# A two-layer transformer block on one core: the first layer's GpSimd work moved to VectorE and TensorE, and its bias table built from bfloat16 parts

## The chip, the cores and the metric

One core of a Trainium2 chip. The metric is the device time of one execution in microseconds (us); the kernel before has a median of 1634.03 us over 3 runs (1628.46 to 1635.84). A measurement of this kernel can tell about 0.5% (8 us) from no change.

## The reference

512 tokens of width 1024, two layers. What matters here, per layer:

```python
h = rmsnorm(x, norm_mix[l]);  proj = h @ w_in[l]
ua, cq, ckv, kr, qc, kc, vc, ud = jnp.split(proj, IN_SPLITS, axis=-1)
ya = conformer_conv(ua, ...)        # 31 taps over 512 tokens, 256 channels
yb = mla(cq, ckv, kr, ...)          # rope, causal attention, 4 heads
yc = diff_attention(qc, kc, vc, ..., rel_bias, ...)  # + rel_bias[t5_bucket(rel)]
yd = multiscale_pool(ud, ...)       # mean over windows of 2, 4, 8, 16 tokens, less u
x = x + concat([ya, yb, yc, yd]) @ w_out[l]
x = x + memory_cross_attention(rmsnorm(x), mem, ...)
x = x + conv_glu_ffn(rmsnorm(x), ...)
```

The bias `rel_bias[t5_bucket(rel)]` is the same in both layers. It is a sum of steps: for each of 31 distances at which the bucket changes, the difference of two rows of `rel_bias` times an indicator of 0 or 1.

## The kernel before

Everything is written by hand, engine by engine; each engine runs its own list in order and waits on counters (semaphores). x is kept transposed (channels on partitions) in eight tiles of 128 x 512.

**Matmuls.** A weight chunk `raw` (128 x 1024, two buffers) comes by DMA; ScalarE copies it to `wh` in the rounded type (`hi`, L534), VectorE makes the rest `wl` = raw - wh (`lo`, L888), and `gemm(n, ...)` does three products per 128 rows (L1344, L1346, L1347), 24 matmuls for a chunk n. `x` is split the same way into `a_hi` (ScalarE, L554) and `a_lo` (VectorE, L953). `gemm(n)` needs `lo(n)`, which VectorE does two chunks ahead, right after it has evicted chunk n-2 (`scaled`, L914). Chunks 0 to 14 are the projection, 15 to 30 the keys and values of the memory.

**Start of the first layer.** ScalarE squares the eight tiles of x into two buffers `sqx` (L557), GpSimd adds them up in `ssum` (L508), and TensorE makes the norm of it (`sums_of`, then `row_of` with the inverse root). VectorE makes the angles of rope between its `a_lo` (`reduce_angles`, L1007 to L1017).

**Bias table.** 16 tiles (`bias_tile(s)`, L1412), one after each projection chunk of the first layer. For each, ScalarE (5) and VectorE (3) make eight tiles of indicators 128 x 512 (`indicators`, L567 and L963) in one set of buffers, and TensorE does 8 float32 matmuls, 32 output columns each; four of them stand side by side in the array. One float32 matmul shows as two in the trace. ScalarE evicts the tile (`evict_bias`) and SyncE stores it to DRAM, from where the attention loads it in both layers.

**Projection loop.** For n = 0 to 11, VectorE does `scaled(n)`, `indicators(n + 2)` (first layer), `lo(n + 2)` and a number of the 62 convolution taps (`convolve`, L930, one 128 x 512 operation each). After n = 11 come four `qm` (L1074), which read the products `uq0` to `uq3` (L1377) out of two PSUM banks in turn; `uq1` waits until ScalarE has copied `kr` out (`km`, L642). GpSimd makes the window means of the pool branch (L459 to L480).

**Attention.** Steps t = 0 to 19; step t has scores of tile t (L1502 and L1510), softmax, and `gemm(15 + t)`. VectorE does in step 0 `negatives` (L1100), the remaining taps, then `lo(16)`; in step 1 `negatives`, the normalising, a further `negatives`, then `lo(17)`; and so on. TensorE asks for `lo(16)` at the beginning of step 1, between its scores.

Of the kernel before, what the change touches and what calls it, by code (L numbers as in the profile page):

```python
# [172 lines left out]
def block_program(nc, xT, memT, pos, const, vecs, small, w_first, w_main, w_up, w_down, w_last, out):  # L173
    with ExitStack() as ctx:
# [59 lines left out]
        ptr, _ = sb("ptr", [P, 4, 4, P], F32)  # L234
# [40 lines left out]
        assert at + 32 <= vc_at + 4096  # L275
# [3 lines left out]
        inds = [ering[:, i, :] for i in range(RING)] + [ptr[:, i].rearrange("p k q -> p (k q)") for i in range(2)]  # L279
# [11 lines left out]
        def v(name, j=0, w=1):  # L291
# [7 lines left out]
        bias0_in, mem_out, rope_in, masks = sem("bias0_in"), sem("mem_out"), sem("rope_in"), sem("masks_in")  # L299
        mem_sq, mem_root, mem_scaled = sem("mem_squared"), sem("mem_root"), sem("mem_scaled")  # L300
# [11 lines left out]
            "g_freed_by_act", "v_full", "v_freed_by_dve", "v_freed_by_act", "dve_steps", "pool_steps",  # L312
            "memf_in", "cross_maxima", "root_of_stat", "root_inverted", "gate_out", "pads_zeroed", "glu_done",
# [13 lines left out]
        DVE_INDS = ((0,), (1, 3))  # L327
        ACT_INDS = ((2, 4, 6), (5, 7))
        BIG = 2.0 ** 20

        def layer_program(layer):
# [3 lines left out]
             dve_steps, pool_steps, memf_in, xmax, root, root_inv, gate_out, pads, glu_done, cq_sq, m_hi, m_lo,  # L335
# [32 lines left out]
            def sync(sp):  # L368
# [56 lines left out]
                for n in range(4, 35):  # L425
# [3 lines left out]
                    if first and n == 12:  # L429
                        sp.wait_ge(mem_scaled, KT)  # L430
                        sp.dma_start(mem_norm, memf[:]).then_inc(mem_out, 16)
# [11 lines left out]
            def gpsimd(pool):  # L443
                step = Steps(pool, pool_steps)

# [6 lines left out]
                pool.wait_ge(pads, 2)  # L452

                def window_sums(i):

                    pool.wait_ge(g_dve, 8 + i)
                    u = ud[:, i, :]

                    step(pool.tensor_tensor(psa[:, 0:526], u[:, 1:527], u[:, 0:526], ALU.add))  # L459
                    if i == 0:  # L460
                        step(pool.tensor_tensor(psb[64:P, 0:524], psa[64:P, 2:526], psa[64:P, 0:524], ALU.add))
                    else:
                        step(pool.tensor_tensor(psb[:, 0:524], psa[:, 2:526], psa[:, 0:524], ALU.add))
                        step(pool.tensor_tensor(psa[:, 0:520], psb[:, 4:524], psb[:, 0:520], ALU.add))
                        step(pool.tensor_tensor(psb[64:P, 0:512], psa[64:P, 8:520], psa[64:P, 0:512], ALU.add))

                def window_differences(i):

                    u = ud[:, i, :]
                    if i == 0:  # L470
                        wins = ((slice(0, 64), psa, 14), (slice(64, P), psb, 12))
                    else:
                        wins = ((slice(0, 64), psa, 8), (slice(64, P), psb, 0))
                    for rows, win, o in wins:
                        inv16 = cst[rows, CCOLS["inv16"] + 16 * i:CCOLS["inv16"] + 16 * i + 16]
                        invw = cst[rows, CCOLS["invw"] + i:CCOLS["invw"] + i + 1]
                        pool.tensor_tensor(win[rows, o:o + 16], win[rows, o:o + 16], inv16, ALU.mult)
                        step(pool.tensor_scalar(win[rows, o + 16:o + S], win[rows, o + 16:o + S], invw, None,
                                                ALU.mult))
                        pool.tensor_tensor(u[rows, PPAD:PPAD + S], win[rows, o:o + S], u[rows, PPAD:PPAD + S],  # L480
                                           ALU.subtract).then_inc(ud_done, 1)
                    pool.wait_ge(ud_done, 2 * i + 2)
# [1398 lines left out]
```

## Time and profile before

| | |
|---|---|
| median of 3 runs | 1634.03 us |
| profiled execution | 1633.34 us, span 1631.6 us |
| TensorE busy | 1581.8 us (97%) |
| VectorE, ScalarE, GpSimd busy | 1024.8, 734.8, 196.9 us |
| mean granted TensorE clock | 0.982 of full |
| first layer, from the start to its attention | about 180 us |
| second layer, projection and attention begin | about 848 us, 954 us |

In the timelines a row merges neighbouring instructions of one line (xcount); "idle before" tells how long the engine had nothing and what released it. An instruction's duration contains its fill and drain, so the pace of a series is the distance of starts. The chain's rows count from the release on, without that overlap. PEclk 1.00 is 2.4 GHz, 0.50 is 1.2 GHz.

### The profile page before, as it was taken

To read this page: it belongs to the slowest core of one execution; us is meant where nothing else is said; L and a number is where in the kernel's file an instruction comes from. 1 tells how busy PE (TensorE), PEld (TensorE's weight loads), DVE (VectorE), ACT (ScalarE), POOL (GpSimd) and SP (SyncE) were. 2 spreads that over 40 slices of the span, in tenths; PEclk is the share of its full clock that TensorE was granted. 3 is DMA by queue.
4 is the path that set the end of the run, shared out by engine and by line. 5 is a ranking of instruction groups with operands and counts; after the bars stand their busy time and mean duration, and the time that the engine had idled before them with its cause. 6 is when DMAs were issued, how large, how long until landed. Compare 5 with 4: busy or idle time off the path is not lost.

```text
span 1631.6 us, 21648 instructions
## 1 busy us (share of the span) xinstructions
PE 1581.8 (97%) x7790; PEld 1229.9 (75%) x7790; DVE 1024.8 (63%) x1539; ACT 734.8 (45%) x1142; POOL 196.9 (12%) x140
## 2 busy tenths in 40 slices
PE   5999999999999999999999999999999999999997
PEld 3673677787688888888878677768768888888886
DVE  6698876543447746745767997654344773674574
ACT  6774767432444423423453266743244441442342
POOL 2050014220030000000021402422002000000002
PEclk7997999999999999999999999999999999999998
DMA  5232332132022323232243133212202323232322
GB/s 185 98 117 65 110 117 89 49 103 91 13 91 93 101 91 103 90 104 90 90 139 115 65 102 112 98 52 91 90 14 90 104 90 103 91 103 90 98 83 90
DMA packets 45437, 151.29 MB, mean 93 GB/s; under 512 B 5040, under 2 KB 5296, under 8 KB 44720
## 3 DMA queue, kind: packets, MB, share of 16 engines
q1 hardware_dynamic: 45360, 150.24, 27.8%
q8 instruction: 52, 0.85, 0.2%
q14 instruction: 25, 0.20, 0.0%
HBM read 142.88 MB, written 7.34 MB: 92 GB/s over the span
## 4 chain that ended last, share of the span: by engine, by line
PE 91%; DVE 4%; ACT 3%; issue 1%; DMA 1%; SPq 0%; DVEq 0%; ACTq 0%
PE psum L1344 25%; PE psum L1346 25%; PE psum L1347 25%; PE psum L1377 4%; PE psum L1524 2%; PE psum L1535 2%; PE psum L1502 2%; PE psum L1510 2%; PE psum L1412 2%; PE psum L1386 1%; PE psum L1398 1%; ACT wh L534 1%; DVE wl L888 1%; PE psum L1657 1%; ACT ering L806 0%
## 5 line engine op out<-in xcount | busy, mean ns | idle before, releaser
L534 ACT ACTIVATE wh<-raw 128x1024 fp32r<-128x1024 f32 x226 | 239.4, 1059 | 584.1 <-PE psum L1347 571.7
L1344 PE MATMUL psum<-a_hi,wh 128*128 128x512 f32 x1072 | 425.2, 397 | 10.2 <-DVE a_lo L953 10.1
L1346 PE MATMUL psum<-a_lo,wh 128*128 128x512 f32 x1072 | 420.6, 392 | 0.0
L1347 PE MATMUL psum<-a_hi,wl 128*128 128x512 f32 x1072 | 420.4, 392 | 0.0
L888 DVE TENSOR_TENSOR wl<-raw,wh 128x1024 fp32r<-128x1024 f32 x222 | 273.5, 1232 | 130.4 <-ACT wh L534 130.1
L1344 PEld LDWEIGHTS psum<-a_hi,wh 128*128 128x128 f32 x1072 | 203.4, 190 | 64.5 <-DVE a_lo L953 11.8
L1344 PE MATMUL psum<-b_hi,wh 128*128 128x512 f32 x608 | 240.4, 395 | 8.2 <-DVE x_sb L1222 4.4
L1347 PE MATMUL psum<-b_hi,wl 128*128 128x512 f32 x608 | 236.8, 389 | 0.0
L1346 PE MATMUL psum<-b_lo,wh 128*128 128x512 f32 x608 | 236.8, 389 | 0.0
L1347 PEld LDWEIGHTS psum<-a_hi,wl 128*128 128x128 f32 x1072 | 203.2, 190 | 43.3
L1346 PEld LDWEIGHTS psum<-a_lo,wh 128*128 128x128 f32 x1072 | 203.5, 190 | 41.1
L1222 DVE TENSOR_TENSOR x_sb<-x_sb,psum 128x512 f32<-128x512 f32 (+1 forms) x80 | 54.9, 686 | 170.6 <-PE psum L1347 170.6
L1344 PEld LDWEIGHTS psum<-b_hi,wh 128*128 128x128 f32 x608 | 114.1, 188 | 37.4 <-issue 6.5
L1347 PEld LDWEIGHTS psum<-b_hi,wl 128*128 128x128 f32 x608 | 114.1, 188 | 24.2
L1346 PEld LDWEIGHTS psum<-b_lo,wh 128*128 128x128 f32 x608 | 114.2, 188 | 23.8 <-issue 1.0
L914 DVE TENSOR_TENSOR up<-psum,rbc 128x512 f32<-128x512 f32 x88 | 60.9, 692 | 89.3 <-PE psum L1347 84.6
L930 DVE SCALAR_TENSOR_TENSOR acc<-conv_in,vec,acc 128x512 f32<-128x512 f32 x120 | 98.7, 822 | 3.4
L508 POOL TENSOR_TENSOR ssum<-ssum,sqx 128x512 f32<-128x512 f32 x48 | 78.8, 1642 | 132.4 <-ACT sqx L557 131.5
L505 POOL COPY ssum<-sqx 128x512 f32<-128x512 f32 x7 | 4.9, 705 | 734.0 <-ACT sqx L557 734.0
L1344 PE MATMUL psum<-mems,wh 128*128 128x256 f32 x256 | 80.7, 315 | 0.8 <-DVE wl L888 0.8
L495 POOL TENSOR_TENSOR wl<-raw,wh 128x1024 fp32r<-128x1024 f32 x20 | 47.8, 2392 | 205.5 <-ACT wh L534 204.3
L1347 PE MATMUL psum<-mems,wl 128*128 128x256 f32 x256 | 72.2, 282 | 0.0
(207 smaller groups left out, 2011.8 us busy)
## 6 DMA issues: line engine op xcount, KB each, us to landing
raw<-in_w_main SPq DMA_DIRECT2D x106, 512.0 KB, 3.3
raw<-in_w_up SPq DMA_DIRECT2D x88, 512.0 KB, 3.2
raw<-in_w_down SPq DMA_DIRECT2D x32, 512.0 KB, 3.2
raw<-in_w_last SPq DMA_DIRECT2D x16, 384.0 KB, 3.0
bias_scratch<-ptr SPq DMA_DIRECT2D x16, 256.0 KB, 3.4
bias<-bias_scratch SPq DMA_DIRECT2D x16, 256.0 KB, 3.9
sw<-in_small SPq DMA_DIRECT2D x2, 1152.0 KB, 6.4
raw<-in_w_first SPq DMA_DIRECT2D x4, 512.0 KB, 4.9
```

Of the source, the lines that this page charges most:

```text
L495: pool.tensor_tensor(wl[:, slot(n % 2)].rearrange("p k m -> p (k m)"), raw[:, slot(n % 2), :], wh[:, slot(n % 2)].rearrange("p k m -> p (k ...
L508: pool.tensor_tensor(ssum[:], ssum[:], sqx[:, k % 2, :], ALU.add).then_inc(ss_in, 1)
L534: act.activation(wh[:, slot(b)].rearrange("p k m -> p (k m)")[:, 0:width], raw[:, slot(b), 0:width], ACT.Copy).then_inc(w_hi, 1)
L888: dve.tensor_tensor(wl[:, slot(b)].rearrange("p k m -> p (k m)"), raw[:, slot(b), :], wh[:, slot(b)].rearrange("p k m -> p (k m)").bitcast ...
L914: dve.tensor_tensor(dst, G[slot(b)], rbc[:], ALU.mult).then_inc(g_dve, 1)
L930: ins = dve.scalar_tensor_tensor(acc[:, i, :], win, w, acc[:, i, :], ALU.mult, ALU.add)
L1222: dve.tensor_tensor(x_sb[:, at, :], x_sb[:, at, :], G[slot(b)].rearrange("p (o s) -> p o s", o=1), ALU.add).then_inc(g_dve, 1)
L1344: pe.matmul(out_ap, wh[:, slot(b), k, :], his[:, k, :], start=((begin or first) and i == 0), stop=False)
L1346: pe.matmul(out_ap, wh[:, slot(b), k, :], los[:, k, :], start=False, stop=False)
L1347: last = pe.matmul(out_ap, wl[:, slot(b), k, :], his[:, k, :], start=False, stop=(end and i == len(tiles) - 1))
L1377: last = pe.matmul(ps[rows, cols], lhs, rhs, start=(i == 0), stop=(i == len(pairs) - 1))
L1412: last = pe.matmul(SC[s % 2][32 * j:32 * j + 32, :], lf[:, 32 * odd:32 * odd + 32], inds[2 * j + odd], start=(odd == 0), stop=(odd == 1))
```

## The change

First layer and both layers' pool branch:

1. GpSimd no longer adds the squares of the first norm. TensorE adds each `sqx` tile by a float32 product with the identity into PSUM (`V[1]`), between the tiles of `gemm(0)`; ScalarE copies the sum out.
2. The window means go from GpSimd to VectorE, in both layers (`pool_window`, in n = 9 and 10), with scaling and subtraction in one operation.
3. The table `lf` is split into three bfloat16 parts, whose sum is exact; the indicators are bfloat16 too. `bias_tile` does 3 x 8 bfloat16 matmuls in place of 8 float32 ones. Two sets of indicators are kept, so tile s waits for tile s-2 only.
4. VectorE makes 6 of 8 indicators in tiles 0 to 2, 3 in tiles 3 to 9, 2 in tiles 10 to 15; ScalarE the others.
5. `reduce_angles` goes out of the start into n = 4 to 7; the memory's norm from n = 6 and 7 to n = 10 and behind `indicators(14)`; its store on SyncE's queue from chunk 12 to chunk 16. ScalarE does the two functions that go with them after the roots of n = 8, where it loads its tables anyway.
6. The convolution's taps are spread anew over n = 2 to 11, the `qm`, and the attention's steps 0 to 3.

```diff
 def indicators(s):                      # VectorE; ScalarE likewise
-        if s > 0:
-            dve.wait_ge((ind_used, b_full)[odd], s)
-        for g in DVE_INDS[odd]:
+        if s > 1:
+            dve.wait_ge((ind_used, b_full)[odd], s - 1)
+        for g in DVE_INDS[s][odd]:
...
-DVE_INDS = ((0,), (1, 3))
+DVE_INDS = [((0, 2, 4), (1, 3, 5))] * 3 + [((0,), (1, 3))] * 7 + [((0,), (1,))] * 6
...
 def bias_tile(s):
-        for j in range(4):
-            last = pe.matmul(SC[s % 2][32 * j:32 * j + 32, :], lf[:, 32 * odd:32 * odd + 32],
-                             inds[2 * j + odd], start=(odd == 0), stop=(odd == 1))
+        for part in range(3):
+            for j in range(4):
+                last = pe.matmul(SC[s % 2][32 * j:32 * j + 32, :],
+                                 lf_parts[:, part, 32 * odd:32 * odd + 32],
+                                 inds[8 * (s % 2) + 2 * j + odd], start=(odd == 0 and part == 0),
+                                 stop=(odd == 1 and part == 2))
...
-    bias_tile(1)
-    gemm(0, 0, a_hi, a_lo, ready=lambda i: pe.wait_ge(x_lo, i + 1))
-    pe.wait_ge(ss_in, KT)
+    for k in range(KT):
+        gemm(0, 0, a_hi, a_lo, tiles=range(k, k + 1), ready=lambda i: pe.wait_ge(x_lo, i + 1),
+             begin=(k == 0), end=(k == KT - 1))
+        pe.wait_ge(sq_in, k + 1)
+        pe.matmul(V[1], ident, sqx[:, k % 2, :], start=(k == 0), stop=(k == KT - 1)).then_inc(ss_in, 1)
+        if k == 3:
+            bias_tile(1)
+    gemm(1, 1, a_hi, a_lo, tiles=range(2), end=False)
+    pe.wait_ge(first_ss, 1)
     sums_of("stat_mix", (ssum, one))
...
-    if n >= 2:
-        convolve({2: 2, 3: 2, 8: 7, 9: 2, 10: 3, 11: 3}.get(n, 4))
+    if n in (9, 10):
+        pool_window(n - 9)
...
+    if n >= 2 and first:
+        convolve({2: 3, 3: 3, 4: 3, 5: 8, 6: 4, 7: 4, 8: 4, 9: 2, 10: 3, 11: 0}[n])
+    elif n >= 2:
+        convolve({2: 3, 3: 3, 4: 5, 5: 5, 6: 5, 7: 5, 8: 8, 9: 1, 10: 1, 11: 1}[n])
...
-    convolve(2 if h < 3 else 16)
+    convolve((1 if h < 3 else 0) if first else (2 if h < 3 else 12))
...
-                        convolve(len(taps))
+                        convolve(len(taps) - 9 if first else len(taps))
+                    if 1 <= t < 4:
+                        convolve(3)
```

On VectorE at the start of the first layer, before the change, behind the first indicators (`rtmp` and `turns` are the angles, `wl` is `lo`):

```order
L963 TENSOR_SCALAR ering<-posf,cst 128x512 x3
L953 SCALAR_TENSOR_TENSOR a_lo<-x_sb,cst,a_hi 128x512
L1007 TENSOR_SCALAR rtmp<-posf,cst 64x512
L1008 TENSOR_SCALAR turns<-rtmp,cst 64x512
L953 SCALAR_TENSOR_TENSOR a_lo<-x_sb,cst,a_hi 128x512
L1010 TENSOR_SCALAR turns<-turns 64x512
L1011 TENSOR_SCALAR turns<-turns 64x512
L953 SCALAR_TENSOR_TENSOR a_lo<-x_sb,cst,a_hi 128x512
L1014 SCALAR_TENSOR_TENSOR rtmp<-turns,rtmp 64x512 x3
L953 SCALAR_TENSOR_TENSOR a_lo<-x_sb,cst,a_hi 128x512
```

The same place after the change, from the first indicators on (the line numbers are those of the changed kernel; `ind_a` and `ind_b` are the indicators):

```order
L960 TENSOR_SCALAR ind_a<-posf,cst 128x512 x6
L862 TENSOR_TENSOR wl<-raw,wh 128x1024
L927 SCALAR_TENSOR_TENSOR a_lo<-x_sb,cst,a_hi 128x512 x2
L960 TENSOR_SCALAR ind_a<-posf,cst 128x512 x2
L960 TENSOR_SCALAR ind_b<-posf,cst 128x512
L960 TENSOR_SCALAR ind_a<-posf,cst 128x512 x2
L960 TENSOR_SCALAR ind_b<-posf,cst 128x512
L927 SCALAR_TENSOR_TENSOR a_lo<-x_sb,cst,a_hi 128x512 x6
L862 TENSOR_TENSOR wl<-raw,wh 128x1024
```

The seven operations on angles have left this place, and three more indicators stand in each of the first tiles.

On VectorE at the first layer's attention, steps 0 and 1, before (the ISA rows are the `negatives`, `acc` the convolution):

```order
L914 TENSOR_TENSOR vct<-psum,rbc 128x512
L1150 SCALAR_TENSOR_TENSOR lam<-lam,vec 128x1
L930 SCALAR_TENSOR_TENSOR acc<-conv_in,vec,acc 128x512 x2
L888 TENSOR_TENSOR wl<-raw,wh 128x1024
L1100 ISA dring,mins<-psum,bias_98 128x512
L1107 RECIPROCAL rec<-sums 128x2
```

and after:

```order
L888 TENSOR_TENSOR vct<-psum,rbc 128x512
L1159 SCALAR_TENSOR_TENSOR lam<-lam,vec 128x1
L904 SCALAR_TENSOR_TENSOR acc<-conv_in,vec,acc 128x512 x9
L862 TENSOR_TENSOR wl<-raw,wh 128x1024
L1109 ISA dring,mins<-psum,bias_98 128x512
L904 SCALAR_TENSOR_TENSOR acc<-conv_in,vec,acc 128x512 x3
L1116 RECIPROCAL rec<-sums 128x2
```

Nine taps now stand ahead of `lo(16)` in step 0 where two stood, and three more in each of steps 1 to 3. In the second layer four stand in step 0, none behind it.

## Rows read from the trace of the kernel before

**Rows 1.** The page: the chain that ended last, shares by engine.

```profile
PE 91%; DVE 4%; ACT 3%; issue 1%; DMA 1%; SPq 0%; DVEq 0%; ACTq 0%
```

**Rows 2.** Chain in order of time, first layer: start, us, what.

```profile
41.35 0.23 PE psum L1347
42.95 1.85 PE psum L1412 x16
...
149.56 3.57 PE psum L1412 x16
```

**Rows 3.** Timeline, GpSimd then VectorE, 16 to 33 us: start, us, what, idle before.

```profile
16.40 11.03 POOL L508 TENSOR_TENSOR ssum<-ssum,sqx 128x512 f32<-128x512 f32 x7 [0.46 <-ACT sqx L557]
...
22.96 5.01 DVE L1014 SCALAR_TENSOR_TENSOR rtmp<-turns,rtmp 64x512 f32<-64x512 f32 x3
...
29.83 2.74 DVE L953 SCALAR_TENSOR_TENSOR a_lo<-x_sb,cst,a_hi 128x512 fp32r<-128x512 f32 x4
```

**Rows 4.** Who waited for whom, 0 to 300 us, TensorE: us, times, longest.

```profile
PE psum L1344 <- DVE a_lo L953: 10.1, 5, 4.2
...
PE psum L1377 <- ACT km L642: 2.2, 1, 2.2
```

**Rows 5.** Timeline, VectorE: the first indicators, and sixteen taps.

```profile
7.13 1.46 DVE L963 TENSOR_SCALAR ering<-posf,cst 128x512 f32<-128x512 f32 x3
...
150.64 12.56 DVE L930 SCALAR_TENSOR_TENSOR acc<-conv_in,vec,acc 128x512 f32<-128x512 f32 x16
```

**Rows 6.** Timeline: weight loads of a bias tile, small matmuls, a table load.

```profile
12.18 0.15 PEld L1412 LDWEIGHTS psum<-ering,lf 128*32 128x32 f32 x4 [2.49 <-DVE ering L963]
...
216.40 1.09 PE L1535 MATMUL psum<-ptr,vm 128*64 128x128 f32 x16
...
36.82 1.28 ACT L543 ACT_TABLE_LOAD   x1
```

**Rows 7.** Timeline, VectorE, start of the first layer's attention.

```profile
183.61 1.54 DVE L930 SCALAR_TENSOR_TENSOR acc<-conv_in,vec,acc 128x512 f32<-128x512 f32 x2
185.06 1.22 DVE L888 TENSOR_TENSOR wl<-raw,wh 128x1024 fp32r<-128x1024 f32 x1
...
192.78 1.23 DVE L888 TENSOR_TENSOR wl<-raw,wh 128x1024 fp32r<-128x1024 f32 x1 [2.92 <-ACT wh L534]
...
213.76 0.69 DVE L1100 CUSTOM_DVE_ANT_0 dring<-psum,bias 128x512 f32<-128x512 f32 x1 [2.33 <-PE psum L1502]
```

**Rows 8.** Timeline, TensorE, the same stretch.

```profile
186.34 0.38 PE L1344 MATMUL psum<-mems,wh 128*128 128x256 f32 x1
...
194.06 0.38 PE L1344 MATMUL psum<-mems,wh 128*128 128x256 f32 x1 [0.80 <-DVE wl L888]
...
212.46 1.13 PE L1502 MATMUL psum<-qk 32*128 32x512 f32 x4
```

**Rows 9.** Busy us and granted clock (PEclk) by stretch.

```profile
20.00:30.00 10.00, 2.96 (x7) 1.67 (x6) 9.73 (x9) 8.98 (x14) 6.85 (x5) 0.50 0.00 0
...
137.00:154.00 17.00, 16.54 (x30) 3.91 (x31) 10.71 (x16) 0.41 (x1) 0.00 (x0) 0.51 0.13 42
...
922.00:937.00 15.00, 13.73 (x30) 4.37 (x31) 14.39 (x20) 4.53 (x7) 0.00 (x0) 1.00 0.11 35
```

**Rows 10.** Timeline, VectorE then TensorE, second layer.

```profile
893.72 4.12 DVE L930 SCALAR_TENSOR_TENSOR acc<-conv_in,vec,acc 128x512 f32<-128x512 f32 x4
...
900.56 9.27 DVE L930 SCALAR_TENSOR_TENSOR acc<-conv_in,vec,acc 128x512 f32<-128x512 f32 x7
...
921.04 0.69 DVE L914 TENSOR_TENSOR qk<-psum,rbc 128x512 f32<-128x512 f32 x1 [0.61 <-PE psum L1347]
...
925.62 0.69 DVE L1074 TENSOR_TENSOR qm<-psum,rope 128x512 f32<-128x512 f32 x1
...
959.12 1.22 DVE L888 TENSOR_TENSOR wl<-raw,wh 128x1024 fp32r<-128x1024 f32 x1
...
960.39 0.39 PE L1344 MATMUL psum<-mems,wh 128*128 128x256 f32 x1
```

More of the change, by code:

```diff
@@ L326, in block_program, with made @@
         TILES = 16
-        DVE_INDS = ((0,), (1, 3))
-        ACT_INDS = ((2, 4, 6), (5, 7))
+        DVE_INDS = [((0, 2, 4), (1, 3, 5))] * 3 + [((0,), (1, 3))] * 7 + [((0,), (1,))] * 6
+        ACT_INDS = [tuple(tuple(g for g in range(odd, 8, 2) if g not in dve[odd]) for odd in range(2))
+                    for dve in DVE_INDS]
+        def made(groups, s, odd):
+            return sum(len(r) for tile in groups[:s] for r in tile) + sum(len(r) for r in groups[s][:odd + 1])
         BIG = 2.0 ** 20
@@ L428, in sync @@
                             store_bias(s)
-                    if first and n == 12:
+                    if first and n == 16:
                         sp.wait_ge(mem_scaled, KT)
@@ L451, in gpsimd @@
                 pool.memset(ud[:, :, 0:PPAD], 0.0).then_inc(pads, 1)
[L452 to L482, printed above, removed]
                 def upper(n):
@@ L508, in sum_squares @@
                             pool.tensor_tensor(ssum[:], ssum[:], sqx[:, k % 2, :], ALU.add).then_inc(ss_in, 1)
-                if first:
-                    sum_squares(0)
-                for i in range(2):
-                    window_sums(i)
-                    window_differences(i)
                 for n in POOL_LO:
@@ L601, in scalar @@
                         split_x(i, 0, c("g0", i))
+                        if i == 1:
+                            indicators(1)
+                        if i == 3:
+                            evict_bias(0)
+                    hi(1)
                     evict_bias(1)
-                    hi(1)
+                    act.wait_ge(ss_in, KT)
+                    act.activation(ssum[:], V[1], ACT.Copy).then_inc(first_ss, 1)
                     indicators(2)
-                if first:
                     hi(2)
@@ L639, in scalar @@
                         roots("stat_kv", c("eps6"), 1.0 / P)
+                        if first:
+                            act.wait_ge(mem_sums, 1)
+                            act.activation(mroot[:], TR[0][:, 0:M], ACT.Sqrt, bias=c("eps6"),
+                                           scale=1.0 / D).then_inc(mem_root, 1)
+                            act.wait_ge(angles, 1)
+                            act.activation(rope[64:P, :], turns_all[64:P, :], ACT.Sin).then_inc(rope_in, 1)
                 ps = v_wait("kr")
@@ L1043, in vector @@
                     lo(n + 2)
-                    if first and n == 6:
+                    if first and 4 <= n < 8:
+                        reduce_angles(n - 4)
+                    if first and n == 10:
                         dve.wait_ge(mem_root, 1)
                         step(dve.reciprocal(mroot[:], mroot[:]))
-                    if first and 6 <= n < 8:
-                        for k in range(4 * n - 24, 4 * n - 20):
-                            dve.tensor_tensor(memf[:, k, :], memf[:, k, :], mroot[:], ALU.mult).then_inc(mem_scaled, 1)
+                    if n == 9:
+                        latents()
+                    if n in (9, 10):
+                        pool_window(n - 9)
                     if n in (1, 3):
@@ L1418, in tensor @@
                     pe.matmul(TR[1][:, 0:1], rel_rows[:], ones[:, 0:1], start=True, stop=True).then_inc(rel_full, 1)
[L1419 removed]
+                    pe.wait_ge(tab_in, 4)
                     bias_tile(0)
[L1421 to L1423 removed]
+                    for k in range(KT):
+                        gemm(0, 0, a_hi, a_lo, tiles=range(k, k + 1), ready=lambda i: pe.wait_ge(x_lo, i + 1),
[6 more added lines that the diff above has]
+                    pe.wait_ge(first_ss, 1)
                     sums_of("stat_mix", (ssum, one))
[L1425 removed]
+                    gemm(1, 1, a_hi, a_lo, tiles=range(2, 6), begin=False, end=False)
                     row_of("stat_mix")
[L1427 removed]
+                    gemm(1, 1, a_hi, a_lo, tiles=range(6, KT), begin=False)
                     bias_tile(2)
```

82 lines of the change are left out of this document (49 added, 33 removed).

## The prediction

> **What bounds the kernel now.** The page first: TensorE holds 91% of the chain that ended last [rows 1], and is busy 97% of the span. So an edit counts where it shortens TensorE's own list, ends one of its waits or makes a new one, or moves its clock; what VectorE, ScalarE or GpSimd save elsewhere is free. Then who waited for whom: of the first 300 us TensorE spent 10.1 us waiting for `a_lo`, all in the first 31 us, and 2.2 us once for ScalarE's copy of `kr` [rows 4]. Then the timelines of those places. At the start VectorE is late because the angles stand between its `a_lo`, and three of them take 5.01 us while GpSimd adds squares; the same kind of operation takes 2.74 / 4 = 0.69 us once GpSimd is still [rows 3]. Last the clock: it was at half (1.2 GHz) in the starved start, and again from 137 to 154 us after the 2.2 us gap at `kr`, where the second layer, without a gap, runs the same products at full clock [rows 4, 9].
>
> **The start of the first layer.** Before, TensorE begins `bias_tile(2)` at 42.95 us [rows 2]. After, on VectorE: its table is ready at 7.1 us, when the first indicators start [rows 5], and the three parts are five small dependent operations, some 1.1 us; six indicators at 1.46 / 3 = 0.49 us each [rows 5], 11.1 us; `lo(0)` 1.2, two `a_lo` 1.4, six indicators 2.9: 16.6 us. Then `a_lo` comes each 0.7 us (ScalarE, about 1.1 us a tile, is a little slower), and TensorE becomes the slowest: three products of 0.23 [rows 2] and a float32 product with the identity, which is two instructions of (1.85 - 0.13) / 4 = 0.43 us [rows 2] (the 1.85 us are four groups, and I take 0.13 us for the turn into them), so 1.55 us for each of tiles 2 to 7, and one `bias_tile`: from 17.3 to 28.2 us. Two tiles of `gemm(1)`, the sums, four tiles: 33.1 us. Beside them ScalarE copies the sum (28.8), makes two indicators and `hi(2)` (31.2), loads a table in 1.28 us [rows 6] and takes the root; the row is ready at about 33.2. Row and last two tiles: `bias_tile(2)` at 35.7 us. **Gain 7.2 us.** If the clock stays at half for another window of this stretch it is 4, and at best 8.
>
> **The bias tiles.** One costs 1.85 us at full clock and 3.57 at half [rows 2]. After: 24 bfloat16 matmuls, four abreast, so six groups. This is not in the trace. Below it is bounded by streaming: half a float32 instruction each, 6 x 0.215 + 0.13 = 1.42 us. Above, by the nearest row for small matmuls side by side, 16 in 1.02 us of pace (1.09 with the drain), 64 ns each [rows 6]: 24 x 0.064 + 0.13 = 1.66 us. I take 1.50, nearer to streaming since these are four times as long as those. Tiles 2 to 12, 14 and 15 stand in the path at full clock: 13 x 0.35 = **4.6 us gained** (2.5 to 5.6); tile 13 at half clock 0.8. ScalarE has one more indicator (0.7 us) in tiles 10 to 15; ahead of the `kr` copy that costs 0.5 us of the path. In the loop VectorE has 7.1 us a chunk. It comes late at n = 5 (8 taps) and n = 6 to 8 (angles, 4 taps), by up to 5 us, but `lo(n + 2)` has a chunk in hand and is just in time, and the wait for the norms of n = 9 lets it catch up. `pool_window` is about 3.6 and 5.0 us at 0.7 us an operation; with it `qm(0)` ends 10 us after chunk 11 where it ended 8, which the half clock in `uq1` hides. To the attention: -7.2 - 4.6 - 0.8 + 0.5 = **-12.1 us**.
>
> The Trainium skill ("TensorE: Matmul & The Clock Gate", Part 3, "The mechanism") says that weight loads overlap running matmuls only when they are for other rows of the array; all of these use the same rows. By it each of the six groups would pay its loads. The trace speaks against it: in the float32 tile, four groups of 0.43 us leave 0.13 of 1.85 us for all loads [rows 2].
>
> **The taps left for the attention.** This is the term against the change. Of 62 taps, 44 stand ahead of the attention in the first layer after, 60 before. A tap is 12.56 / 16 = 0.78 us [rows 5]. In step 0 nine taps in place of two stand ahead of `lo(16)`: its end goes from 186.3 to 191.7 us on the old time scale, and TensorE began `gemm(16)` at 186.34, right on it [rows 7, 8]. So TensorE waits 5.4 us. Steps 1 to 3 have three more taps each, 7.0 us, ahead of `p_ready` and of `negatives`, on which the next scores wait. VectorE had 3.1 us of waits in step 1 (2.92 for a weight tile [rows 7]) and nothing in 2 and 3, so it is 5.4 + 7.0 - 3.1 = 9.3 us late at step 4; I take 0.6 us off because TensorE's own list ran a little behind VectorE there, so step 5's scores come 8.7 us later than 212.46 [rows 8]. From there TensorE is the slower again (VectorE waited 2.33 us at 213.76 [rows 7]), so nothing is given back. The 5.4 us gap also lets the clock fall, as in the start [rows 9]: about 2 us of matmul time that the VectorE chain doesn't cover. **Loss 10.7 us** (5 if TensorE's and VectorE's queues interlock more loosely than I follow them, 13 at most).
>
> **Second layer.** No bias tiles, so only costs. VectorE's taps from n = 4 to 11 are 31 before and after. The windows add 8.6 us there; GpSimd's absence gives back the stretch (seven taps in 9.27 us against 5.5, four in 4.12 against 3.1, some 6 us in all) and the 0.61 us of waiting at 921.04 [rows 10]. So `qm(0)`, at 925.62 and on the path, is 2.0 us later. In step 0 four taps in place of two: `lo(16)` ends at 961.8, TensorE wanted it at 960.39 [rows 10]: 1.4 us. **Loss 3.4 us** (2 to 4.5).
>
> **Sum.** -12.1 + 10.7 + 3.4 = +2.0 us, on the profiled execution's 1633.34: 1635.3 us. That execution is 0.7 us under the median of 1634.03, so 1635 as it stands. Other moves are free: the memory's norm, its store in front of chunk 16's load on SyncE's queue (`hi(16)` comes only behind the split of the memory), two table loads less on ScalarE under a busy TensorE.
>
> **Rivals.**
> - *The clock stays up at `kr` (20%).* The gap there is 2.2 us before and by my count 3.0 after; whether the clock falls after a gap of this size depends on where it lies: it fell in the first layer. If not, the 17 us at half clock [rows 9], nearly all matmul time, become half as long: about 8 us. 1627 us.
> - *The taps are hidden (12%).* If TensorE has more to do in steps 0 to 3 than waits, or VectorE catches up, only about 1 of the 10.7 us stays: 1625 us.
> - *A new fall in the second layer (15%).* The later `qm(0)` opens a gap of 2.6 us between `uq1` and `uq2`, where the clock was 1.00 [rows 9]. At half clock the products there cost about 4 more: 1639 us.
> - *The bfloat16 tiles are slower (8%).* If the loads of each group don't hide, the tile costs 6 x (0.215 + 0.15) + 0.13 = 2.3 us, the 0.15 being four weight loads of such a tile [rows 6]. Then 13 x 0.8 us turn the sum: 1646 us, slower. The tiles cost time from 1.85 us each on; from 2.0 us each the whole is slower by more than 0.5%.
> - *As summed (45%).* 1635 us, 1630 to 1641.
>
> **How the numbers follow.** 0.5% is 8 us, what a measurement of this kernel can tell; the bounds are 1625.9 and 1642.2. Faster: most of the taps' case (0.09), not quite half of the clock's (0.09), and 0.06 from both terms of the start and tiles at their better ends: 0.24. Slower: the tiles' case (0.08), a third of the new fall (0.04), 0.02 else: 0.14. Same 0.62. The range reaches from the taps' case with a better start, 1621, to the tiles' case, 1646.
>
> **What would show it.** `bias_tile(2)` at 34 to 38 us, its duration 1.4 to 1.7 us; no wait for `a_lo` above 2 us; the first layer's first scores near 167.5 us; a wait of TensorE for `wl` of about 5 us in step 1, with PEclk 0.5 behind it; the distance from step 0's to step 5's scores 43 us where it was 32.6; VectorE idle in front of scaled(12). In the second layer, from the first projection chunk to the first scores 2 us more. The prediction is wrong if TensorE doesn't wait at `gemm(16)`, if the clock is up from `kr` on, or if a bias tile costs as much as before.

## The result and the profile after

The changed kernel has a median of 1638.31 us (1634.98 to 1639.54, 10 runs), the kernel before 1634.60 us in the same comparison (10 runs): ratio 1.0024, interval 1.0013 to 1.0035. A second comparison, with 6 runs, gave 1639.17 us and 1.0038 (1.0022 to 1.0054). So it is 4 to 6 us slower, within the 0.5% that the prediction calls no change. The profiled execution took 1634.98 us, the quickest of its runs, with a span of 1633.2 us beside 1631.6.

The page of the changed kernel, engines and chain, beside [rows 1]:

```profile
PE 1580.6 (97%) x7934; PEld 1233.4 (76%) x7934; DVE 1018.3 (62%) x1583; ACT 730.5 (45%) x1137; POOL 140.1 (9%) x96
...
PE 90%; DVE 6%; ACT 2%; issue 1%; DMA 0%; DVEq 0%; SPq 0%; ACTq 0%
```

VectorE's share of the chain is 6% where it was 4%: work was moved to VectorE, and TensorE now waits for it more. Who waited for whom on TensorE, 0 to 300 us (us, times, longest), beside [rows 4]:

```profile
PE psum L1355 <- DVE wl L862: 5.6, 1, 5.6
PE psum L1388 <- ACT km L616: 3.3, 1, 3.3
...
PE psum L1521 <- DVE mins L1109: 2.1, 2, 1.6
PE psum L1355 <- DVE a_lo L927: 0.8, 2, 0.4
```

The 10.1 us for `a_lo` are 0.8. In their place stand 5.6 us for `wl` (that is `lo(16)`), 2.1 for `negatives`, and 3.3 at `kr` where it was 2.2. TensorE's timeline at the start, then at `lo(16)` and step 3, then in the second layer:

```profile
24.49 1.02 PE L1438 MATMUL psum<-sqx,cst 128*128 128x512 f32 x2
...
26.05 1.02 PE L1438 MATMUL psum<-sqx,cst 128*128 128x512 f32 x2
...
35.97 1.48 PE L1423 MATMUL psum<-ind_a,lf_parts 128*32 128x512 bf16 x24
37.38 0.50 PE L1355 MATMUL psum<-a_hi,wh 128*128 128x512 f32 x1
...
176.46 0.58 PE L1355 MATMUL psum<-mems,wh 128*128 128x256 f32 x1 [5.62 <-DVE wl L862]
...
190.94 1.58 PE L1521 MATMUL psum<-qk 32*128 32x512 f32 x4 [1.63 <-DVE mins L1109]
...
922.10 8.09 PE L1388 MATMUL psum<-cq,sw 128*128 128x512 f32 x8 [2.56 <-DVE qm L1080]
...
961.06 0.39 PE L1355 MATMUL psum<-mems,wh 128*128 128x256 f32 x1 [1.52 <-DVE wl L862]
```

The identity products come every 1.56 us. `bias_tile(2)` begins at 35.97 us and the next product at 37.38: 1.41 us of path for a tile, where the timeline before has 1.86. And the granted clock (PEclk, third number from the end) by stretch, beside [rows 9]:

```profile
20.00:30.00 10.00, 10.00 (x54) 5.54 (x52) 5.09 (x8) 6.51 (x11) 0.00 (x0) 1.00 0.07 15
99.00:113.00 14.00, 14.00 (x105) 10.29 (x104) 13.63 (x24) 11.84 (x17) 0.00 (x0) 1.00 0.37 133
123.00:140.00 17.00, 16.62 (x39) 4.47 (x40) 10.56 (x22) 0.32 (x1) 0.00 (x0) 0.51 0.17 47
172.00:182.00 10.00, 5.54 (x21) 4.17 (x21) 9.65 (x18) 2.85 (x6) 0.00 (x0) 0.66 0.39 129
896.00:908.00 12.00, 12.00 (x62) 10.17 (x62) 11.46 (x19) 1.32 (x2) 0.00 (x0) 1.00 0.39 132
920.00:932.00 12.00, 9.90 (x11) 2.63 (x12) 9.30 (x14) 0.00 (x0) 0.00 (x0) 0.58 0.13 44
```

1.00 in the start, where it was 0.50; half behind the gap at `kr` as before; 0.66 around the new wait at `lo(16)`; and 0.58 in the second layer where it was 1.00. VectorE at the first layer's attention, beside [rows 7]:

```profile
168.09 7.05 DVE L904 SCALAR_TENSOR_TENSOR acc<-conv_in,vec,acc 128x512 f32<-128x512 f32 x9
175.18 1.22 DVE L862 TENSOR_TENSOR wl<-raw,wh 128x1024 fp32r<-128x1024 f32 x1
```

Nine taps, 7.05 us, then `lo(16)`.

The milestones of TensorE's list, in us (the second execution of the changed kernel is from the second comparison):

| | before | after | after, second |
|---|---|---|---|
| `bias_tile(2)` | 42.88 | 35.97 | 35.74 |
| norm sums of n = 9 | 101.08 | 90.41 | 90.17 |
| row of n = 9 | 113.21 | 99.36 | 100.75 |
| first layer's first scores | 179.83 | 164.31 | 165.62 |
| its step 5 | 212.46 | 207.38 | 208.62 |
| second layer's sums of n = 9 | 895.99 | 892.53 | 893.80 |
| its `kr` product | 920.86 | 914.19 | 915.46 |
| its first scores | 953.91 | 953.02 | 955.92 |
| span | 1631.6 | 1633.2 | 1637.7 |

15.5 us ahead at the first scores, 5.1 at step 5, 0.9 at the second layer's first scores, 1.6 behind at the end. Two of the places behind step 5 stand in the last term of the account below.

### The profile page after: what moved, and what is told of

Read it like the earlier page. It is cut to its first block, busy times and chain, and to the rows that moved or that the text cites. A ratio compares the mean times of both kernels' runs of the same rounds, so it can differ in the third digit from the quotient of the medians.

```text
span 1633.2 us, 21919 instructions
## 1 busy us (share of the span) xinstructions
PE 1580.6 (97%) x7934; PEld 1233.4 (76%) x7934; DVE 1018.3 (62%) x1583; ACT 730.5 (45%) x1137; POOL 140.1 (9%) x96
## 4 chain that ended last, share of the span: by engine, by line
PE 90%; DVE 6%; ACT 2%; issue 1%; DMA 0%; DVEq 0%; SPq 0%; ACTq 0%
PE psum L1355 25%; PE psum L1358 24%; PE psum L1357 24%; PE psum L1388 4%; PE psum L1543 2%; PE psum L1554 2%; PE psum L1521 2%; PE psum L1529 2%; DVE acc L904 1%; PE psum L1423 1%; PE psum L1397 1%; DVE wl L862 1%; PE psum L1409 1%; ACT wh L506 1%; PE psum L1676 1%
## 5 line engine op out<-in xcount | busy, mean ns | idle before, releaser
L904 DVE SCALAR_TENSOR_TENSOR acc<-conv_in,vec,acc 128x512 f32<-128x512 f32 x120 | 90.1, 750 | 3.5
L1355 PE MATMUL psum<-mems,wh 128*128 128x256 f32 x256 | 81.8, 319 | 7.1 <-DVE wl L862 7.1
L485 POOL TENSOR_TENSOR ssum<-ssum,sqx 128x512 f32<-128x512 f32 x41 | 69.8, 1702 | 133.7 <-ACT sqx L529 133.7
L1357 PE MATMUL psum<-mems,wh 128*128 128x256 f32 x256 | 73.0, 285 | 0.0
```

What stands on the lines that cost most here:

```text
L485: pool.tensor_tensor(ssum[:], ssum[:], sqx[:, k % 2, :], ALU.add).then_inc(ss_in, 1)
L904: ins = dve.scalar_tensor_tensor(acc[:, i, :], win, w, acc[:, i, :], ALU.mult, ALU.add)
L1355: pe.matmul(out_ap, wh[:, slot(b), k, :], his[:, k, :], start=((begin or first) and i == 0), stop=False)
L1357: pe.matmul(out_ap, wh[:, slot(b), k, :], los[:, k, :], start=False, stop=False)
```

## The experiments

Each was timed against runs of the kernel before on the same chip, and the ratio is to these. Two runs that weren't on the same chip are better compared by their ratios than by their medians; where the two ways differ, both are given. The diffs are against the changed kernel where not said otherwise.

**The changed kernel again** (`after_again`).

> The changed kernel itself, once more, on the same chip as the other three of this row and against the same runs of the kernel before. Theory A: its ratio is again 1.001 to 1.0035 and it is 3 to 5 us slower than before. Theory B: the first comparison took it at its dear end, since lo_first, whose trace ends at the same time (span 1633.1 us), came out at 0.9992: then the ratio is 0.999 to 1.001.

1639.17 us, ratio 1.0038 (1.0022 to 1.0054), 6.2 us: theory A's side, a little above its figures (1.001 to 1.0035, 3 to 5 us). It also shows how far executions of one program lie apart: the same instructions from the sums of n = 9 to the row took 8.95 us in one and 10.58 in the other (the kernel before: 12.13). The instructions are the same; the granted clock is 1.00 throughout in the one and half for a part in the other.

**lo(16) first** (`lo_first`).

```diff
+                        lo(N_WK + 1)
                         convolve(len(taps) - 9 if first else len(taps))
...
-                    if t < 7:
+                    if 0 < t < 7:
                         lo(N_WK + 1 + t)
```

> The changed kernel, with lo(16) moved ahead of step 0's taps in both layers (nine taps in the first, four in the second) and nothing else. Theory A (my prediction's): TensorE's wait of 5.6 us for lo(16) is only where VectorE's lateness shows first; the same nine taps still stand ahead of step 1's negatives, so TensorE does gemm(16) at once and then waits for VectorE in step 1 or 2 instead. Of the 10.4 us that steps 0 to 5 lost, at most 2 to 3 come back (a shorter single gap, perhaps no fall of the clock); second layer up to 1.5. The whole is 1 to 5 us faster than the changed kernel. Theory B: the loss is the order, lo(16) behind the taps; then nearly all comes back, 5.6 us of wait and 2 us of clock in the first layer and 1.5 in the second: 8 to 10 us faster than the changed kernel, and the distance from step 0's scores to step 5's is below 36 us.

TensorE's timeline in step 1:

```profile
178.76 2.04 PE L1530 MATMUL psum<-km,qm 128*128 128x512 f32 x2 [4.69 <-DVE mins L1109]
```

The wait of 5.62 us for `wl` is gone and one of 4.69 us for `negatives` (`mins`) stands a few products further on. The distance from step 0's scores to step 5's is 42.13 us, where it was 43.07: theory A for the place. In the second layer the wait of 1.5 us shrinks to 0.59. The median is 1634.09 us, ratio 0.9992 (0.9979 to 1.0006): 4 to 5 us better than the changed kernel by the medians, 5 to 8 by the ratios, so more than the 1 to 5 of A and less than the 8 to 10 of B. The profiles tell where it is, beside `after_again`, whose span is 4.6 us longer: 0.9 us in the first layer's attention; 2.3 us behind the first scores of the second (955.92 to 970.72 us there, 953.30 to 965.81 here), with a granted clock of 1.00 for 0.91 from 956 to 966 us; and 1.6 us in each layer at a gap of 2.2 us that both have, where the clock falls in `after_again` and not here. Some of this is lost again towards the end. Beside the first profile of the changed kernel, whose clock didn't fall at `lo(16)`, the second layer's part is 0.75 us, not 2.3. So 1.6 to 3.2 us are gained where the edit moves something; the rest is where the clock fell, and whether the edit has a part in that stays open.

**Taps ahead of the attention** (`taps_ahead`).

```diff
-                    convolve((1 if h < 3 else 0) if first else (2 if h < 3 else 12))
+                    convolve((1, 3, 3, 0)[h] if first else (2 if h < 3 else 12))
...
-                    convolve(4)
+                    convolve(11)
                 scaled(12, places[12])
...
-                convolve(3)
+                convolve(5 if first else 3)
                 scaled(13, places[13])
...
-                        convolve(len(taps) - 9 if first else len(taps))
-                    if 1 <= t < 4:
+                        convolve(len(taps) - 3 if first else len(taps))
+                    if t == 1:
                         convolve(3)
```

> The changed kernel, first layer only: 13 of the 18 taps left for the attention go to where VectorE is idle ahead of it (2 more behind each of qm(1) and qm(2), 7 more ahead of scaled(12), 2 more ahead of scaled(13)); step 0 has two taps as in the kernel before, step 1 three. Theory A: the taps left for the attention are the whole of the 10.4 us, and the idle time of 2.7, 5.9 and 2.1 us there takes them: the distance from step 0's scores to step 5's goes from 43.1 to 33 or 34 us (three taps in step 1 meet VectorE's old wait of 2.9 us), first scores not later than 164.3 + 1 us; the whole 8 to 11 us faster than the changed kernel, so about 6 to 9 us faster than the kernel before. Theory B: part of the 10.4 us is something else (the bias tiles' order, the memory's norm, its store on SyncE's queue), and then the distance stays above 36 us, or the first scores come more than 2 us later.

TensorE's timeline, the scores of steps 0, 2 and 5:

```profile
165.49 1.13 PE L1521 MATMUL psum<-qk 32*128 32x512 f32 x4
...
177.81 1.13 PE L1521 MATMUL psum<-qk 32*128 32x512 f32 x4 [0.40 <-DVE mins L1109]
...
197.59 1.13 PE L1521 MATMUL psum<-qk 32*128 32x512 f32 x4
```

32.10 us from step 0 to step 5, no wait there above 0.40 us, and the first scores at 165.49, with `after_again` at 165.62: theory A, by a little more than it had (33 to 34 us). 1627.6 us, ratio 0.9954 (0.9936 to 0.9972), 11 to 12 us better than the changed kernel by the medians, 11 to 14 by the ratios. The thirteen taps, 10 us of VectorE, cost nothing where they went.

**The gap at kr filled** (`kr_filled`).

```diff
                 for h in range(4):
                     product(f"uq{h}", (sw[:, SW_UQ0 + P * h:SW_UQ0 + P * h + P], cq[:, 0, :]),
                             (sw[0:64, SW_UQ1 + P * h:SW_UQ1 + P * h + P], cq[0:64, 1, :]))
+                    if h == 0:
+                        gemm(12, 0, a_hi, a_lo, free="in")
...
-                gemm(12, 0, a_hi, a_lo, free="in")
```

> The changed kernel, both layers: gemm(12) stands between uq0 and uq1 instead of behind the small products, so that TensorE has 5.5 us of work while ScalarE copies kr and VectorE comes to qm(0). Theory A: it is these gaps (3.3 us in the first layer, 2.6 in the second) that let the clock fall behind them; without them it stays at 1.00 through the small products. First layer 3.3 + about 8 us, second 2.6 + about 4: 14 to 18 us faster than the changed kernel, some 1621 to 1624. Theory B: the clock falls for the small products themselves (four float32 products that change their weights each time, at a busy share below the rest): then only the gaps are saved, 4 to 6 us.

Clock by stretch:

```profile
123.00:140.00 17.00, 15.63 (x64) 6.46 (x62) 14.07 (x28) 4.46 (x9) 0.00 (x0) 1.00 0.16 46
140.00:156.00 16.00, 12.62 (x78) 8.21 (x79) 7.60 (x10) 12.66 (x18) 0.00 (x0) 0.79 0.38 130
911.00:925.00 14.00, 14.00 (x41) 6.88 (x40) 11.93 (x21) 2.20 (x2) 0.00 (x0) 1.00 0.16 57
```

TensorE's waits from 100 to 215 us:

```profile
PE psum L1423 <- ACT ind_a L539: 4.7, 2, 3.5
```

ScalarE's timeline:

```profile
134.13 0.59 ACT L619 ACTIVATE km<-psum 64x512 f32<-64x512 f32 x1 [10.96 <-PE psum L1388]
...
139.73 4.33 ACT L539 ACTIVATE ind_a<-posf,edge,slope 128x512 bf16<-128x512 f32 x6
```

The clock is 1.00 through the small products in both layers, with the same products as before: the gap was what let it fall, theory A. Second layer: from the `kr` product to the first scores 32.90 us for 38.83. First layer: 43.66 for 47.50, less than expected, because `bias_tile(14)` now stands right behind the small products, without `gemm(12)`'s 5.5 us ahead of it, and waits for ScalarE's indicators (4.7 us in two waits), which ScalarE begins only at 139.73, after having waited 10.96 us for the products behind `kr`; the clock falls behind that gap (0.79). 1630.16 us, ratio 0.9978 (0.9965 to 0.9990): 8 to 10 us for the 14 to 18 of theory A. Its account of the clock holds, its time doesn't.

**Second layer's last taps moved** (`second_taps`).

```diff
-                        convolve({2: 3, 3: 3, 4: 5, 5: 5, 6: 5, 7: 5, 8: 8, 9: 1, 10: 1, 11: 1}[n])
+                        convolve({2: 3, 3: 3, 4: 5, 5: 5, 6: 5, 7: 5, 8: 8, 9: 0, 10: 0, 11: 0}[n])
...
-                    convolve((1 if h < 3 else 0) if first else (2 if h < 3 else 12))
+                    convolve((1 if h < 3 else 0) if first else (2 if h < 3 else 15))
```

> The changed kernel, second layer only: the taps of n = 9, 10 and 11 (one each) go behind qm(3), so VectorE reaches qm(0) 2.3 us earlier. Theory A: the gap between uq1 and uq2 was 2.56 us and made the clock fall; now it is 0.3 to 1 us and the clock stays at 1.00: second layer's attention begins 2 + 4 = 5 to 6 us earlier than in the changed kernel, the whole 4 to 6 us faster. Theory B: the clock falls there for another reason (where it falls differs between executions of one kernel); then about 2 us.

TensorE's timeline, the small products of the second layer:

```profile
917.32 8.67 PE L1388 MATMUL psum<-cq,sw 128*128 128x512 f32 x16
...
928.15 2.83 PE L1388 MATMUL psum<-ckv,sw 128*64 128x512 f32 x6 [1.04 <-DVE qm L1080]
```

All four `uq` run in one piece, 8.67 us at full clock; the only gap is 1.04 us behind them, as in the kernel before. From the `kr` product to the first scores 32.91 us for 38.83: theory A. 1632.44 us, ratio 0.9992 (0.9979 to 1.0005), 5 to 8 us better than the changed kernel.

**The kernel before with the bfloat16 tiles alone** (`before_bf16`; diff against the kernel before; the table is split as in the change).

```diff
-                        for j in range(4):
-                            last = pe.matmul(SC[s % 2][32 * j:32 * j + 32, :], lf[:, 32 * odd:32 * odd + 32],
-                                             inds[2 * j + odd], start=(odd == 0), stop=(odd == 1))
+                        for part in range(3):
+                            for j in range(4):
+                                last = pe.matmul(SC[s % 2][32 * j:32 * j + 32, :],
+                                                 lf_parts[:, part, 32 * odd:32 * odd + 32],
+                                                 inds[2 * j + odd], start=(odd == 0 and part == 0),
+                                                 stop=(odd == 1 and part == 2))
```

> The kernel before, with nothing of the change but the bias tiles: the table in three bfloat16 parts, indicators in bfloat16, 24 bfloat16 matmuls for 8 float32 ones, one set of indicators as before. Theory A: the tile itself is shorter, 1.40 us of path for 1.85 at full clock, whatever stands around it: 13 x 0.43 + 0.8 at half clock = 6.4 us gained up to the attention, 1.1 us lost at the start for making the parts; the whole 4 to 6 us faster than the kernel before. Theory B: with one set of indicators tile s waits for the engines that fill the set, so a shorter tile only waits longer: the matmuls take 1.4 us and the gain is under 2 us.

TensorE's timeline, the first tile behind the start, and the second layer's small products:

```profile
43.31 1.48 PE L1421 MATMUL psum<-ind_a,lf_parts 128*32 128x512 bf16 x24
44.72 0.50 PE L1352 MATMUL psum<-a_hi,wh 128*128 128x512 f32 x1
...
919.18 8.08 PE L1385 MATMUL psum<-cq,sw 128*128 128x512 f32 x8 [2.39 <-DVE qm L1082]
```

The tile takes 1.41 us of path here too, with one set of indicators, and the first scores come at 173.20, 6.6 us sooner. Of these 1.5 are a shorter fall of the clock at n = 9 (10.61 us from the sums to the row for 12.13); the other 5.1 are theory A's part up to the attention (6.4 - 1.1). The whole gained only 2.7 us by the medians and 3.4 by the ratio, less than the 4 to 6 of A: 1630.22 us, ratio 0.9979 (0.9970 to 0.9988). In the profile the rest went in the second layer, whose program is that of the kernel before: from its sums of n = 9 to its first scores 61.92 us, where it was 57.92, with a gap of 2.39 us that wasn't there. But the profiled execution, 1632.28 us, is the slowest of the eleven, so how often this happens isn't shown.

**The sums back on GpSimd** (`gpsimd_sums`).

```diff
+                if first:
+                    sum_squares(0)
...
-                        pe.wait_ge(sq_in, k + 1)
-                        pe.matmul(V[1], ident, sqx[:, k % 2, :], start=(k == 0), stop=(k == KT - 1)).then_inc(ss_in, 1)
...
-                    act.wait_ge(ss_in, KT)
-                    act.activation(ssum[:], V[1], ACT.Copy).then_inc(first_ss, 1)
```

> The changed kernel, with the first norm's squares added up by GpSimd again as in the kernel before; the products with the identity and ScalarE's copy of their sum are left out, all else is as changed. Theory A: the 7 us at the start came from the angles leaving VectorE's list; GpSimd's adding costs 11.03 / 7 = 1.58 us a tile where TensorE's pace is 1.55, and slows VectorE's a_lo, but neither stands alone in the path: bias_tile(2) at 35 to 38 us (35.97 in the changed kernel, 42.95 before), the whole within 2 us of the changed kernel. Theory B: it is GpSimd that makes VectorE late there: bias_tile(2) at 39 us or later, 3 us or more lost.

Timelines of VectorE, GpSimd and TensorE:

```profile
8.43 2.83 DVE L960 TENSOR_SCALAR ind_a<-posf,cst 128x512 bf16<-128x512 f32 x6
...
15.03 2.92 DVE L960 TENSOR_SCALAR ind_a<-posf,cst 128x512 bf16<-128x512 f32 x2
17.88 1.49 DVE L960 TENSOR_SCALAR ind_b<-posf,cst 128x512 bf16<-128x512 f32 x1
...
23.51 4.05 DVE L927 SCALAR_TENSOR_TENSOR a_lo<-x_sb,cst,a_hi 128x512 fp32r<-128x512 f32 x6
...
13.01 10.30 POOL L485 TENSOR_TENSOR ssum<-ssum,sqx 128x512 f32<-128x512 f32 x7
...
40.39 1.48 PE L1423 MATMUL psum<-ind_a,lf_parts 128*32 128x512 bf16 x24
```

Theory A falls, B holds. While GpSimd is still, six indicators take 2.83 us; while it adds, two take 2.92 and one 1.49, three times as much, and six `a_lo` 4.05 once it is done. `bias_tile(2)` comes at 40.39 us, the whole at 1644.28 us, ratio 1.0065 (1.0052 to 1.0079), 5.1 us above `after_again`, which was timed on the same chip. The 4.4 us at `bias_tile(2)` are net: the run also takes the products with the identity off TensorE. The Trainium skill ("SBUF — State Buffer", "Who interferes with whom") says that a VectorE instruction in a two-port mode, or with two inputs from SBUF, and a GpSimd instruction that reads SBUF shut each other out for the whole instruction. The rows agree: a GpSimd addition is 10.30 / 7 = 1.47 us, and each indicator then takes as long as one addition.

**A better version, in three steps.** `best_a` joins `taps_ahead` and `second_taps`.

> The changed kernel with the edits of two runs: the first layer's taps ahead of its attention (taps_ahead) and the second layer's taps of n = 9 to 11 behind qm(3) (second_taps). Theory A: the two lie in different layers and add up: first layer 0 to 5 at 32 us, second layer from the kr product to the first scores at 33 us (38.7 in taps_ahead): 5 to 6 us faster than taps_ahead, near 1622, ratio 0.991 to 0.993 of the kernel before. Theory B: what the second layer gains is mostly where the clock happens to fall; then the ratio stays at that of taps_ahead, 0.995.

1621.48 us, ratio 0.9925 (0.9912 to 0.9939); from `kr` to the second layer's first scores 33.10 us. Theory A, and the parts add up.

`best_b` fills the first layer's gap on top of it (here with the place from which ScalarE's `indicators(14)` was taken, and `gemm(12)`'s old place, which only the second layer keeps):

```diff
                                .broadcast_to([64, 4, S]), ACT.Copy).then_inc(v_act, 1)
+                if first:
+                    indicators(14)
...
                     evict_bias(13)
-                    indicators(14)
...
-                    convolve(11)
+                    convolve(9)
...
-                convolve(5 if first else 3)
+                convolve(7 if first else 3)
...
+                    if first and h == 0:
+                        gemm(12, 0, a_hi, a_lo, free="in")
...
-                gemm(12, 0, a_hi, a_lo, free="in")
+                if not first:
+                    gemm(12, 0, a_hi, a_lo, free="in")
```

> best_a, and in the first layer alone gemm(12) between uq0 and uq1, ScalarE's indicators(14) right behind its copy of kr (where it waited 11 us in kr_filled), and two taps of those ahead of scaled(12) ahead of scaled(13) instead. Theory A: with the gap filled the clock stays at 1.00, so TensorE's work up to the first scores is some 37 us where best_a has 46; but VectorE is idle only 5.2 us of those 46, so it becomes the bound: kr product to first scores 40 to 42 us, 4 to 6 us faster than best_a, near 1616, ratio 0.989 to 0.990. Theory B: VectorE's taps were hidden only by the half clock, and in this order (the taps ahead of scaled(12) and scaled(13)) the gaps come back behind them and the clock falls there: then 0 to 3 us.

Clock by stretch:

```profile
118.00:135.00 17.00, 17.00 (x75) 7.91 (x68) 14.54 (x25) 11.17 (x15) 0.00 (x0) 1.00 0.16 48
135.00:157.00 22.00, 20.25 (x115) 12.41 (x114) 21.40 (x38) 16.72 (x28) 0.00 (x0) 1.00 0.26 96
```

VectorE's timeline, its one wait between 118 us and the first scores:

```profile
129.22 0.69 DVE L1081 TENSOR_TENSOR qm<-psum,rope 128x512 f32<-128x512 f32 x1 [1.98 <-PE psum L1389]
```

The clock stays at 1.00, VectorE is busy all but 1.98 us, and the first scores come 38.16 us behind the `kr` product, where it was 47.50; 40 to 42 were expected. Some of that is given back in the attention, since VectorE is late there: from step 0's to step 5's scores it takes 34.75 us for the 32.02 of `best_a`. 1616.40 us, ratio 0.9897 (0.9876 to 0.9917): 1% better than the kernel before, and theory A.

`best_c` fills the gap in the second layer too, six taps behind `lo(14)`; against `best_b`:

```diff
-                    if first and h == 0:
+                    if h == 0:
                         gemm(12, 0, a_hi, a_lo, free="in")
...
-                    convolve((1, 3, 3, 0)[h] if first else (2 if h < 3 else 15))
+                    convolve((1, 3, 3, 0)[h] if first else (2 if h < 3 else 9))
...
-                convolve(7 if first else 3)
+                convolve(7 if first else 9)
...
-                if not first:
-                    gemm(12, 0, a_hi, a_lo, free="in")
```

> best_b, and gemm(12) between uq0 and uq1 in the second layer too, with six of the fifteen taps behind qm(3) moved behind lo(14). Theory A: in best_a the second layer has no fall of the clock there (its gap is 1.0 us) and VectorE is idle for only some 3 us of the 33, so this is worth 0 to 2 us more than best_b. Theory B: the gap of 1.0 us still costs, by a fall of the clock in some executions: then 3 us or more.

1619.59 us, ratio 0.9912 (0.9892 to 0.9931), not better than `best_b`: neither theory. From the `kr` product to the first scores it takes 31.65 us for 32.91, but the taps put behind `lo(14)` are then in the way of `lo(16)`, for which TensorE waits 3.33 us where it waited 1.50, with a fall of the clock behind it. The two intervals overlap, so it isn't shown to be slower.

## Why the prediction was right, term by term

The time, 1635 us for 1638, and the mechanisms of the first layer held; three terms were off in size or cause and one was missing, and they nearly cancelled. In the profiles the change is +1.6 us for the +2.0 of the sum: -15.5 to the first scores, +10.4 in the attention, +4.1 in the second layer, and +2.5 behind the attentions, for which the sum had nothing (the parts are rounded). That these come so near is luck, and the medians lie further off, at +3.7 and +6.2. The forecast itself starts from the profiled execution; from the median of 1634.03 the same sum gives 1636.

- **Start, 7.2 us: measured 6.9** (42.88 to 35.97). Pace and order were as worked out. What carries it is not only the angles: `gpsimd_sums` gives 4.4 us of it back. No run moves the angles alone, so what they are worth by themselves isn't shown. I had read the slower operations beside GpSimd off the angles (5.01 us for three, [rows 3]) and yet expected `gpsimd_sums` to be harmless: I left out that the second tile's six indicators stand beside GpSimd's work there, while in the kernel before VectorE's three came ahead of it.
- **Bias tiles, 0.35 us each at full clock: measured 0.45**, 13 x 0.45 = 5.9 us for 4.6. 1.41 us is as good as the lower bound of 1.42 I had worked out by streaming; I had taken 1.50. `before_bf16` has the same tile. The rule of the Trainium skill that I had weighed ("TensorE: Matmul & The Clock Gate", Part 3, "The mechanism") doesn't show here: four weight loads a group, all on the same rows, and none appears in the pace.
- **ScalarE's one more indicator, 0.5 us: measured 1.1**, the gap at `kr` being 3.33 us for 2.21. ScalarE comes to its copy 0.7 us later, one indicator; the other 0.4 is that tile 12 is shorter and TensorE stands at the gap sooner, so tile 12 gained nothing. `before_bf16`, with the shorter tile and without the indicator, has a gap of 2.59 us. The clock fell behind it as before; the rival "the clock stays up at kr" didn't come.
- **Left out: the sums of n = 9.** Behind these 24 products the clock falls or not, and for a shorter or a longer time. From them to the row it took 12.13 us before and 8.95 after, 3.2 us that I had not in the sum. So the first scores were 15.5 us sooner, not 12.1: 6.9 + 5.9 + 0.8 (tile 13, at half clock as before) + 3.2 - 1.1 = 15.7. In the twelve profiles of this study the stretch took 8.95 us twice, 10.5 to 10.6 seven times and 12.1 three times, so part of this is the luck of the profiled execution, which was the quickest of its ten.
- **The taps left for the attention, 10.7 us: measured 10.4**, and 10.4 in `after_again`. The wait was 5.62 us for the 5.4 predicted, the distance 43.07 for 43.3. The split was otherwise than predicted: TensorE's idle time in these steps grew by 6.9 us (7.7 for 0.8), where I had 8.7 for VectorE's lateness, and its busy time by 3.5 (35.3 for 31.8), PEclk being 0.88 for 1.00, where I had 2. `taps_ahead` returns 11.0 of it, `lo_first` 0.9: it is VectorE's amount of work ahead of step 4, not the order at `lo(16)`.
- **Second layer, 3.4 us: measured 4.1** (2.6 to the first scores, 1.5 at `lo(16)`), by another way. `qm(0)` came 2.4 us later behind the `kr` product (7.2 for 4.8), near the 2.0 predicted; the step that failed is that this alone is the cost, with the clock held as it was. What the profiles show:

| | n = 9, sums to row | gap ahead of `uq2` | `kr` to first scores |
|---|---|---|---|
| before | 12.08 | none | 33.05 |
| before_bf16 | 8.87 | 2.39 | 40.26 |
| after | 8.87 | 2.56 | 38.83 |
| after_again | 8.86 | 2.56 | 40.46 |
| lo_first | 8.87 | 2.57 | 40.15 |
| taps_ahead | 12.08 | 2.38 | 38.72 |
| gpsimd_sums | 12.04 | 2.36 | 38.70 |
| kr_filled | 8.86 | none | 32.90 |
| second_taps | 10.49 | none | 32.91 |
| best_a | 8.87 | none | 33.10 |
| best_b | 12.00 | none | 32.91 |
| best_c | 12.08 | none | 31.65 |

In the kernel before, a fall at n = 9 cost 3.2 us and, as I read it, gave VectorE time to come up, so that no gap opened at `qm(0)`. The same program without that fall (`before_bf16`) has the gap, and the clock falls there. With the change the gap is there in either case. With a gap, the way to the scores is 5.7 to 7.4 us longer, the gap included. This is the rival "a new fall in the second layer", which had 15% and 4 us: it came in all five profiles that have the change's second layer up to its first scores, and what it costs was covered by the fall that stayed out at n = 9. What the change is worth here depends on that fall. With it (`taps_ahead`, `gpsimd_sums` and before) the change costs 38.7 - 33.05 = 5.7 us. Without it the kernel before would have the gap as well: `before_bf16` takes 40.26 us, the changed kernel 38.83 and 40.46, so the change costs nothing. Which of the two the kernel before does more often isn't known, since only one of its executions was profiled.
- **Behind the attention I had nothing.** From 310 us on the changed kernel lost 1.6 us more, and the same again at the same place of the second layer, around 1095 us; at the very end 0.7 came back. Both times the clock falls behind a gap of 2.2 us that both kernels have. The two stretches before, then after:

```profile
300.00:330.00 30.00, 27.80 (x171) 21.07 (x170) 12.32 (x21) 14.11 (x23) 2.48 (x2) 1.00 0.16 53
...
1090.00:1100.00 10.00, 7.80 (x34) 5.85 (x32) 5.82 (x8) 4.80 (x8) 2.43 (x2) 1.00 0.23 64
```

```profile
300.00:330.00 30.00, 27.81 (x151) 21.47 (x150) 12.17 (x16) 11.96 (x19) 3.76 (x3) 0.94 0.15 53
...
1090.00:1100.00 10.00, 7.81 (x27) 5.67 (x26) 6.08 (x9) 5.17 (x8) 1.76 (x2) 0.83 0.15 52
```

The clock falls at both places in ten of the twelve profiles and at neither in those of the kernel before and of `lo_first`, so the exception is the profile before; why it is one stays open. So does the rest of the 2 to 5 us by which the two comparisons of medians lie above the 1.6 us of the first pair of spans; that the clock fell more often is shown for `after_again` alone (n = 9, 956 to 966 us).

## What to carry to other kernels

Count each engine's work between two points where it has to meet the engine that bounds the kernel, not instruction by instruction: VectorE's taps were free where VectorE was idle and cost their full time, wherever in the list they stood, where it wasn't. A gap on TensorE costs its length and often a fall of the clock behind it; among the small products of the second layer the two together cost two to three times the gap. Fill it with a product that is ready, and see that what stood behind that product is ready sooner as well. And keep GpSimd still while VectorE is on the path beside it: there an instruction of VectorE took two to three times as long.

## What the runs showed of the hardware

- One program's clock differs by execution: behind the same products of one column TensorE ran at full clock, or at half for a shorter or a longer piece (8.9, 10.5 and 12.1 us from the sums to the row). This moved up to 3.2 us in each layer, and the fall behind the 2.2 us gaps another 3.2 us over both. A gain of some 3 us that shows in one pair of profiles can be this alone.
- Gaps of 2.2 to 3.3 us on TensorE were followed by half clock in all profiles that have them in the small products (nine in the first layer, six in the second); gaps of 1.04 us there in none of four. The gap of 1.5 us at `lo(16)` in the second layer was followed by it in three profiles of eight, `after_again` among them and the changed kernel's first not, and the gaps of 2.2 us near 320 and 1095 us in ten profiles of twelve. So the length of a gap alone doesn't decide.
- Four bfloat16 matmuls of 32 columns side by side pass at 0.213 us a group with new weights each time, half of what a float32 group takes.
